# Second mixing stage of a two-block transformer kernel: eight heads' probabilities turned by DMA instead of by TensorE

## The reference

```python
q, k, v, xr, gr, g_attn, g_rnn = jnp.split(proj, offs, axis=-1)
# per head (8 heads, two softmaxes of 64 columns each, values of 128 columns)
logits = einsum('bqhcd,bkhcd->bhcqk', q_blk, k) * scale + bias
p = softmax(where(rel >= 0, logits, -inf))
attn = p[:, :, 0] - lam * p[:, :, 1]
out = einsum('bhqk,bkhe->bqhe', attn, v)
```

## Time and profile before

| | us |
|---|---|
| median of 3 runs (lowest, highest) | 996.47 (995.94, 996.63) |
| the profiled execution | 995.88 |
| its span, first to last instruction | 994.1 |
| busy: PE, DVE, ACT, POOL | 987.6, 682.7, 553.6, 118.6 |
| granted TensorE clock, mean | 1.000 |

### The profile page before, as it was taken

One profiled execution on the slowest core, in us unless ns is written; L12 is line 12 of the kernel. 1 busy time (PEld: TensorE's weight loads), 2 busy tenths in 40 slices (PEclk: granted clock), 3 DMA queues, 4 the chain that ended last, 5 costly groups with the idle time before them and its releaser, 6 DMA issues.

```text
span 994.1 us, 12539 instructions
## 1 busy us (share of the span) xinstructions
PE 987.6 (99%) x4608; PEld 810.6 (82%) x4608; DVE 682.7 (69%) x998; ACT 553.6 (56%) x761; POOL 118.6 (12%) x109
## 2 busy tenths in 40 slices
PE   8999999999999999999999999999999999999998
PEld 7788888888777788888888888888888888888887
DVE  6666566668987667656565678776689767656663
ACT  7444343577665546444444586868885555443542
POOL 0000000022300000000000041169904000000000
PEclk9999999999999999999999999999999999999999
DMA  7987776586444546766666487658555546777761
GB/s 263 284 266 255 234 250 211 193 305 196 140 152 143 169 130 214 227 198 214 211 204 226 156 229 237 176 163 212 151 191 196 202 156 204 228 223 227 226 198 43
DMA packets 165465, 201.44 MB, mean 203 GB/s; under 512 B 55969, under 2 KB 111658, under 8 KB 165290
## 3 DMA queue, kind: packets, MB, share of 16 engines
q1 hardware_dynamic: 164826, 200.69, 64.3%
q10 hardware_dynamic: 592, 0.14, 0.1%
HBM read 182.45 MB, written 5.77 MB: 189 GB/s over the span
## 4 chain that ended last, share of the span: by engine, by line
PE 96%; DVE 2%; ACT 1%; POOL 1%; issue 0%; ACTq 0%; POOLq 0%; DVEq 0%
PE bank L1969 23%; PE bank L1971 23%; PE bank L1970 23%; PE bank L2087 7%; PE bank L2086 7%; PE bank L2085 7%; PE bank L1984 1%; PE bank L2136 1%; PE bank L2251 1%; DVE lo L1348 0%; PE bank L2151 0%; PE bank L2138 0%; PE bank L2374 0%; PE bank L2375 0%; PE bank L2347 0%
## 5 line engine op out<-in xcount | busy, mean ns | idle before, releaser
L1969 PE MATMUL bank<-hi,xh 128*128 128x512 f32 (+1 forms) x944 | 374.8, 397 | 0.9 <-DVE lo L1574 0.8
L1971 PE MATMUL bank<-hi,xl 128*128 128x512 f32 (+1 forms) x944 | 367.2, 389 | 0.0
L1970 PE MATMUL bank<-lo,xh 128*128 128x512 f32 (+1 forms) x944 | 366.5, 388 | 0.0
L1331 DVE TENSOR_TENSOR lo<-raw,hi 128x2048 fp32r<-128x2048 f32 (+1 forms) x111 | 253.9, 2289 | 146.2 <-ACT hi L824 146.2
L824 ACT ACTIVATE hi<-raw 128x2048 fp32r<-128x2048 f32 (+1 forms) x114 | 216.5, 1901 | 133.7 <-PE bank L2087 97.0
L1969 PEld LDWEIGHTS bank<-hi,xh 128*128 128x128 f32 x944 | 177.3, 188 | 39.7 <-issue 2.5
L1971 PEld LDWEIGHTS bank<-hi,xl 128*128 128x128 f32 x944 | 177.2, 188 | 37.2
L1970 PEld LDWEIGHTS bank<-lo,xh 128*128 128x128 f32 x944 | 177.5, 188 | 34.4
L1348 DVE TENSOR_TENSOR lo<-raw,hi 128x1024 fp32r<-128x1024 f32 (+1 forms) x108 | 131.9, 1230 | 43.1 <-ACT hi L833 42.4
L2085 PE MATMUL bank<-hi,hh 128*128 128x512 f32 (+1 forms) x306 | 119.3, 390 | 0.0
L2087 PE MATMUL bank<-hi,hl 128*128 128x512 f32 (+1 forms) x306 | 118.7, 388 | 0.0
(11 more groups left out here) (271 smaller groups left out, 961.6 us busy)
## 6 DMA issues: line engine op xcount, KB each, us to landing
raw<-in_w_in SPq DMA_DIRECT2D x48, 1024.0 KB
raw<-in_ffn_w_gu SPq DMA_DIRECT2D x82, 512.0 KB
raw<-in_ffn_w_down SPq DMA_DIRECT2D x22, 1024.0 KB
raw<-in_w_up SPq DMA_DIRECT2D x16, 1024.0 KB
raw<-in_w_down SPq DMA_DIRECT2D x16, 1024.0 KB
raw<-in_w_out SPq DMA_DIRECT2D x8, 1024.0 KB
distance_table<-ftab SPq DMA_DIRECT2D x8, 576.0 KB
raw<-in_w_proj_attn SPq DMA_DIRECT2D x4, 1024.0 KB
```

Source lines behind the costliest of these rows:

```text
L1331: nc.vector.tensor_tensor(lo[s][:, :, 0:width], raw[s][:, :, 0:width], hi[s][:, :, 0:width].bitcast(F32), ALU.subtract).then_inc(lo_done, 1)
L1969: nc.tensor.matmul(o, sh, wh, start=first and j == 0, stop=False)
L1970: nc.tensor.matmul(o, sh, wl, start=False, stop=False)
L1971: ins = nc.tensor.matmul(o, sl, wh, start=False, stop=last and j == 3)
```

## The change

The three transposes per head leave TensorE. In list `M2_STEP[2h+1] + 3`, behind the half of the weight, ScalarE splits the joined probabilities of head h into planes (128 x 768 words of 16 bits, from `l2[:, 0, h % 3]` to `l2[:, 1, h % 3]`). SP issues one DMA transpose per head, behind the load of a named unit, back into `l2[:, 0, h % 3]`; it waits there for the planes. In list `M2_STEP[2h+1] + 5`, behind the half of the weight, VectorE merges the turned planes into `pt2[:, h % 2]`. ScalarE's copy from `PT` goes. The products with the values move from portions 18, 21, 24, 27, 30, 32, 35, 38 to 21, 24, 26, 29, 32, 34, 37, 39 (`M2_PV`), and ScalarE's drains to lists 22, 25, 27, 30, 33, 35, 38, 39 (`M2_O`). Lines below the new ones have moved: L1348 is L1371 there, L504 is L516, L1969 is L2000.

```diff
@@ -108,6 +108,10 @@
 M2_STEP = [12, 13, 15, 16, 18, 19, 21, 22, 24, 25, 26, 27, 29, 30, 32, 33]
 M2_PLANES = {4: (0, 0), 5: (0, 1), 16: (3, 0), 17: (3, 1)}
 M2_MERGE = {8: 0, 20: 3}
+M2_P_PLANES = [p + 3 for p in M2_STEP[1::2]]
+M2_P_MERGE = [p + 5 for p in M2_STEP[1::2]]
+M2_PV = [21, 24, 26, 29, 32, 34, 37, 39]
+M2_O = [22, 25, 27, 30, 33, 35, 38, 39]
 M2_RI = 37
 M2_SUB = 39
 M2_DECAY = [48, 49]
@@ -321,6 +325,14 @@
             words = (rg if c == 0 else grt)[:, 4:8, :].rearrange("p b c -> p (b c)")
             return words.bitcast(U16).rearrange("p (k c) -> p k c", c=SEQ)
+        def p_planes_of(h):
+            return l2[:, 1, h % 3, :].bitcast(U16)
+        def p_turned_planes_of(h):
+            return l2[:, 0, h % 3, :].bitcast(U16).rearrange("p (k c) -> p k c", c=P)
         lamv = pt2[:, 0, 0:4 * HD].rearrange("p (a b) -> p a b", b=HD)
@@ -675,11 +687,21 @@
                     sp_eng.dma_start_transpose(q_turned_planes_of(c)[:, :, t * P:(t + 1) * P],
                                                q_planes_of(c)[:, t, :]).then_inc(ffns[1].flip[t], 16)
+            def flip_probabilities(h):
+                sp_eng.wait_ge(k_pt, h + 1)
+                if h >= 2:
+                    sp_eng.wait_ge(k_ptc, h - 1)
+                sp_eng.dma_start_transpose(p_turned_planes_of(h), p_planes_of(h)).then_inc(ffns[0].flip[h % 2], 16)
             for c, (first, _) in enumerate(IN2):
                 for half in range(2):
                     if half == 1 and by_dma(c - 3):
                         flip_mixed(c - 3)
                     columns(a["w_in_2"], U_M2 + 2 * c + half, first, half)
+                    for h in range(NH):
+                        if 2 * c + half == (M2_P_PLANES[h] - 1) // 2 + 5:
+                            flip_probabilities(h)
                 if c in (3, 6):
                     flip_queries(c - 3)
                 if c == 2:
@@ -1190,12 +1212,7 @@
                     nc.scalar.activation(k_2[:, 4 * (cc // 3):4 * (cc // 3) + 4, rows], view, ACT.Copy,
                                          scale=cols[:, C_GAIN + 5:C_GAIN + 6]).then_inc(k_trev, 1)
                 for h in range(NH):
-                    if M2_STEP[2 * h + 1] + 4 == p:
-                        act.wait_ge(k_pt, h + 1)
-                        if h >= 2:
-                            act.wait_ge(k_pv, h - 1)
-                        nc.scalar.activation(pt2[:, h % 2, :], PT[:, 0:SPAN], ACT.Copy).then_inc(k_ptc, 1)
-                    if M2_STEP[2 * h + 1] + 5 == p:
+                    if M2_O[h] == p:
                         act.wait_ge(k_pv, h + 1)
                         for tt, o in ((1, O[h % 2][:, P:SEQ]), (0, O[h % 2][:, 0:P])):
                             ins = nc.scalar.activation(xn[:, tt, h * P:(h + 1) * P], o, ACT.Copy,
@@ -1265,6 +1282,12 @@
                     act.wait_ge(k_xc, b + 1)
                     nc.scalar.activation(xrt[:, b, 0:SEQ], rg[:, b, :], ACT.Tanh, scale=sp[:, 3, b:b + 1])
                 mixing_split(split_hi_part, U_M2, p)
+                h = at(M2_P_PLANES, p)
+                if h >= 0:
+                    act.wait_ge(k_comb, h + 1)
+                    nc.scalar.activation(p_planes_of(h).rearrange("p (s c) -> p s c", s=2),
+                                         l2[:, 0, h % 3, :].bitcast(U16).rearrange("p (c s) -> p s c", s=2),
+                                         ACT.Copy).then_inc(k_pt, 1)
                 if u == 1 and by_dma(c):
                     act.wait_ge(k_ev, 2 * c + t + 1)
@@ -1803,7 +1826,7 @@
                     h, half = k // 2, k % 2
                     dve.wait_ge(k_s, k + 1)
                     if h >= 3:
-                        dve.wait_ge(k_pt, h - 2)
+                        dve.wait_ge(k_ptc, h - 2)
                     if k == 0:
                         dve.wait_ge(bias_2_in, 16)
                     logits(S[k % 2], l2[:, half, h % 3, :], (bias_2[:, h, :], bias_2[:, h, P:SEQ]), k, k_l)
@@ -1874,6 +1897,14 @@
                                           turned_planes_of(cc, tt).rearrange("p (s k) c -> p s k c", s=2)
                                           ).then_inc(k_trev, 1)
                 mixing_split(split_lo_half, U_M2, p)
+                h = at(M2_P_MERGE, p)
+                if h >= 0:
+                    dve.wait_ge(ffns[0].flip[h % 2], 16 * NF1 + 16 * (h // 2) + 16)
+                    if h >= 2:
+                        dve.wait_ge(k_pv, h - 1)
+                    nc.vector.tensor_copy(pt2[:, h % 2, :].bitcast(U16).rearrange("p (k c s) -> p s k c", c=P, s=2),
+                                          p_turned_planes_of(h).rearrange("p (s k) c -> p s k c", s=2)
+                                          ).then_inc(k_ptc, 1)
                 if p in M2_MULT:
                     b = slice(2 * M2_MULT.index(p), 2 * M2_MULT.index(p) + 2)
@@ -2339,15 +2370,7 @@
                         pe.wait_ge(ffns[1].merged, NF1 + 1)
                     pair_scores(q_2, h, k_2, h, k_s)
                 for h in range(NH):
-                    if M2_STEP[2 * h + 1] + 4 == p:
-                        pe.wait_ge(k_comb, h + 1)
-                        if h >= 1:
-                            pe.wait_ge(k_ptc, h)
-                        for j in range(3):
-                            ins = nc.tensor.transpose(PT[:, j * P:(j + 1) * P], l2[:, 0, h % 3, j * P:(j + 1) * P],
-                                                      ident[:, :])
-                        ins.then_inc(k_pt, 1)
-                    if M2_STEP[2 * h + 1] + 5 == p:
+                    if M2_PV[h] == p:
                         pe.wait_ge(k_ptc, h + 1)
                         if h == 0:
                             pe.wait_ge(k_ev, 6)
```

## The result

| | before | changed |
|---|---|---|
| median of 19 runs, us | 996.35 | 997.98 |
| lowest and highest | 995.93, 997.04 (and once 1232.95) | 997.29, 1000.65 |
| ratio, 95% interval | | 1.002 (1.0013 to 1.0026) |
| profiled execution, us | 995.88 | 997.98 |
| its span, us | 994.1 | 996.2 |

The change costs 1.6 us by the medians, 2.0 by the ratio and 1.3 to 2.6 by its interval; 1.0 was forecast (997.5, in a range of 995.0 to 1000.3).

The account below looks back on a forecast made before the run. TensorE, busy 171.93 of 172.00 us in the second mixing stage, was taken as the bound. Its saving of 2.71 us against waits of 0.93, 0.70, 0.3 and 1.8 gave +1.0: 996.47 to 997.5 us, range 995.0 to 1000.3.

Parts of the forecast that it names:

- Gross saving: Second mixing stage: transposes leaving TensorE (2.57) and value products moving (0.14) take 2.71 us off it.
- Portion 21: TensorE's transposes of the keys wait 0.93 us for VectorE's scaled keys: 1.33 + 0.96 less a margin of 1.36.
- Portion 26: TensorE's scores wait 0.70 us for the logits that free the bank: 0.75 + 1.03 less a margin of 1.08.
- Portion 34: Sixth value product waits 0 to 0.65 us, taken as 0.3, for the merge behind VectorE's low half.
- Portion 39: Eighth value product waits 1.8 us for its merge, at the end of a chain from the first gate block.
- block 8's planes: Planes of block c = 8, queued on SP behind the eighth head's transpose: in time or 0.3 us late, counted at portion 39.
- Portion 37: Seventh value product, one of four said to come with a margin: no wait.
- Sum: Over the stage: -2.71 + 0.93 + 0.70 + 0.3 + 1.8 = +1.0 us.
- The cover: Rival, second mixing stage: ScalarE and VectorE follow TensorE's lead, no wait appears, 993.8 us; chance 0.12.
- The SP rival: Eighth head's transpose holds SP, block 8 lands late, portion 39 waits longer: 999.0 to 1000.4 us; chance 0.21.
- GpSimd: Rival: five merges hold GpSimd's convolution, TensorE waits 1.7 us more at the heads' turn, portion 47: 999.2; chance 0.07.

Follow-up runs that it names:

- nothing in the transposes' place: The changed kernel without its planes, SP transposes and merges, value products reading a tile filled once with a constant: 993.40 us, ratio 0.9971 to the kernel before.
- the kernel with the first planes later too: The changed kernel with first, third, sixth, seventh and eighth products, first and third merges, and first head's planes placed later: 994.24 us, ratio 0.9980 to before.

## Why the prediction was right

**Gross saving.** Forecast 2.71 from the spacing of portions in the kernel before, 2.87 with nothing in the transposes' place. Three transposes were 0.36 to 0.38 at the places where they stood alone (0.35 taken), 0.26 beside scores (0.26) and 0.32 ahead of the gate block (0.30); a product was 0.72 alone and 0.63 beside scores, as taken, and 0.63 beside a gate block (0.67). These make up the 0.16. The page of the Trainium skill that spoke against the change (VectorE: DVE Perf Modes, Rules for kernel authors: TensorE for a 128x128 transpose if PSUM will do) has the result on its side here, but not for its figure: 390 ns is given for bf16, 24 times that are 9.4 us, an estimate that no run came near, and the kernel with the first planes later too is faster than the one before with the transposes by DMA.

**Portion 21.** 0.93 forecast, 0.97 measured, which is closer than its terms are. TensorE came 1.36 earlier (1.33 forecast). The scaling of the keys came 0.78 later and not 0.96 (631.72, which is 631.02 without the 0.70, against 630.24): the planes moved VectorE's half by the 0.36 that was taken, but VectorE starts its next operation 0.51 behind the start of the merge (629.69, 630.20), not 0.6, and 0.09 is lost on the way. On the other side, TensorE starts 0.15 behind the end of the scaling (632.40, 632.55), which the sum didn't have. That these cancel is luck. Moving the merge left 0.55 of the wait, moving the planes as well left none.

**Portion 26.** 0.70 forecast, 0.68 measured, behind the third merge and the logits as traced: TensorE came 0.75 earlier, as taken, and the logits 0.96 later, for 1.03.

**Portion 34.** 0.3 forecast, 0.59 measured, inside its ends of 0 to 0.65. Mis-sized: the question was whether VectorE's low half of list 32 moves with TensorE. Without the 0.70 by which the profiled run is late here, it starts at 676.27, against 676.44 in the earlier trace rows: it moved by 0.17 where TensorE came 1.2 earlier. The half before it did move, by 0.87 (672.46 on VectorE, less the 0.70, for 672.63), but from there VectorE works without a pause, 4.51 instead of 3.81. Most of that is the joining of the softmaxes (L1844), two operations that took 1.44 and end as the low half starts; before, the two took 0.90 (row below). In the changed kernel the same two took 0.75 at 627.10, where the convolution doesn't run yet on GpSimd. That it is what makes them longer here wasn't tried.

```profile
675.62 0.90 DVE L1821 SCALAR_TENSOR_TENSOR l<-l,small 128x256 f32<-128x256 f32 x2
```

**Portion 39.** 1.8 forecast, 1.96 measured. The chain is the one that was laid out, but its size is right in part by luck. Laid out it gave a wait of 1.5, and 0.3 was added for block 8's planes, which cost nothing (VectorE was ready 0.17 early). To the start of the product the chain made it 1.82, because the low half took 1.47 for 1.28 and small steps add up to 0.14, among them 0.04 to the first sigmoid and 0.06 from the merge to the product. Spacing adds another 0.14.

**Portion 37.** Nothing was forecast, 0.11 measured: the seventh product was one of the four said to come with a margin, and it hadn't quite one.

**Sum.** -2.87 + 0.97 + 0.68 + 0.59 + 0.11 + 1.96 = +1.44, and the stage of the profiled execution is 1.45 longer. The forecast of +1.0 was 0.4 low: 0.3 at portion 34, 0.2 at 39 and 0.1 at 37, less 0.2 more gross saving. The medians differ by 1.63, 0.2 more than the stage; where that 0.2 is isn't shown, and the lateness ahead of the stage varies by more.

**The rivals.** The cover didn't hold. The SP rival had the right condition (a landing by 691.7 costs nothing): the copy that waits for it started at 692.19, which is 691.5 without the 0.70, and cost nothing. GpSimd did not hold the changed kernel, but it is what is left when TensorE is 2 to 3 us earlier. The 2.10 that the prediction puts down to a copy lies beside a copy of 0.76 and a low half of 1.21 (VectorE, 678.32 and 678.97), and the copy alone isn't long enough for it, since an operation of that form takes 0.48 where nothing holds it up.

## What to carry to other kernels

Where one engine is full, price what leaves it by the spacing of its starts, and then compare, place by place, how long each input had been ready with how much earlier the engine will come plus how much later the input will be: here three waits out of four arose from that sum, and none of them stood in the profile of before. Work that is moved to idle engines is free only at the right place in their lists: the same merges and planes cost 4.3 us in one order and about 0.3 in another. And when waits are taken away one after the other, expect the next margin to give: it took two more moves than planned.

## What the runs showed of the hardware

- VectorE's merge of 128x768 words took 0.58 to 0.62 in 50 of the 56 merges of the seven runs that have them, and 1.12 to 1.15 in six. In all six an addition of GpSimd's convolution (TENSOR_TENSOR) was running as the merge began. In 29 of the 50 it was a multiplication (TENSOR_SCALAR), and there GpSimd came last: the multiplication took 1.74 to 2.02, where the shortest took 0.47, and ended 0.25 to 0.31 behind the merge. In the other 21 no operation of the convolution was running. So either engine can be the one that comes last; where it was VectorE, it lost some 0.55. Why it goes by the operation isn't shown. The eighth merge of the changed kernel, at 696.91, is one of the 29, by GpSimd's timeline:

```profile
696.01 1.74 POOL L805 TENSOR_SCALAR rg<-xrt,cols 128x256 f32<-128x256 f32 x1
```

- A DMA transpose that is issued much earlier need not land much earlier: 4.1 us earlier on SP gave 0.8 earlier at the copy. Which transfers were ahead of it wasn't followed.
- Runs of kernels that are the same up to this stage reach it with up to 1.0 us of difference (-0.09 to 0.93 against the kernel before), which is most of a change of this size; a profiled pair has to be compared from the stage's start.
